# A transformer block with an expert gather: the V row of a step weighed before or after the dense work of that step

## The chip, the cores and the metric

The kernel runs on one core of one Trainium2 chip. The metric is the device time of one execution in microseconds. The kernel before took 2209.41 us, the median of three runs (2208.9 to 2215.3).

## The reference

The program is one residual block over 256 tokens of width 2048, all in float32: a token mixer (stick-breaking attention beside a gated linear recurrence), a layer norm, and then PEER, a channel mixer that picks experts by product keys. Only PEER matters here:

```python
q = (hf @ w_q).reshape(n_tok, PEER_HEADS, 2, PEER_HALF)
half_scores = jnp.einsum('thpd,hpnd->thpn', q, sub_keys)
s_top, i_top = lax.top_k(half_scores, PEER_TOPK)          # 16 of 128, twice
best, pos = lax.top_k(cand, PEER_TOPK)                    # 16 of 256 sums
gates = jax.nn.softmax(best, axis=-1)
act = jnp.einsum('td,thkd->thk', xb, u_tab[ib])           # gather of U rows
w = gb * jax.nn.gelu(act, approximate=False)
out = jnp.einsum('thk,thkd->td', w, v_tab[ib])            # gather of V rows
```

Each of 256 tokens picks 16 of 16384 experts in each of 8 heads. Its output is the sum of the V rows of these experts, weighed by gate times GELU of the product of its own row with the expert's U row. Scaled, the result is added to the residual and normed.

## The kernel before

The span has two parts. Up to about 1000 us come the modulation, the mixer and the query; they are not touched. Then comes the gather stage.

Tokens stand in two blocks of 128, one token to a partition. A *gathered row* is one choice of one head for one block: 128 experts, one per partition, 8 KB each. There are 2 x 8 x 16 = 256 such rows of U and as many of V. A step is named (n, e): n counts the 16 pairs of block and head, e the 16 choices. GpSimd issues the gathers as indirect DMAs (`gather_row`, L543): in step (n, e) the U row (n, e), then the V row (n-1, e). Each kind has a ring of five slots. A U row waits until VectorE has reduced the row that sits in its slot; a V row waits until TensorE has weighed the row in its slot. GpSimd's queue is in order, so a V row that waits holds back the U rows behind it.

VectorE reduces a U row to one number per token (`reduce_row`, L1568, 2.29 us). Once a head's 16 numbers are there, ScalarE takes their GELU (L724) and VectorE multiplies in the gates and spreads the weights over a matrix (`weigh`, L1579). TensorE weighs a V row with four narrow matmuls side by side in the array (`weigh_row`, L1128). At the start of each head it waits for the spread weights (`pe.wait_ge(s_wgt, n)`, L1224), ahead of all the work of that head's steps.

The gather serves only experts of the first 88 of 128 key rows; those of the last 40 key rows are out of the gather's bounds and are computed densely for all tokens. Three kinds of dense work are woven into the steps of TensorE's last loop by tables made from shares:

- `dense_u_piece` (L1150): one quarter of the product of a tile of 128 dense U rows with all tokens. There are 4 x 40 pieces, two in a step from (1,13) to (4,15), about one from (5,0) to (8,11). The tiles come on SP's queue (L491) into two slots. ScalarE takes their GELU (L763, L769).
- `spread_gates` (L1188): one matmul per token that puts its gates into a matrix of dense experts, from a column mask (made for even tokens by ScalarE, L787 and L788, for odd ones by VectorE, L1641) and a row mask (VectorE, L1633). Four tokens in each step from (5,0) to (8,15). Ahead of them stand two transpositions at the start of n = 5 (L1174, L1175), whose result ScalarE copies (L780).
- `dense_v_piece` (L1162): the weighed sum over the dense V rows, from step (9,4) on.

VectorE multiplies the dense activations with these gates (`weigh_dense`, `mix`).

The order of each engine's queue is that in which the code is written. The stretch of TensorE up to step (8,15) is called here the first stretch (n = 1 to 4, dense U pieces alone) and the masked stretch (n = 5 to 8, with gate matmuls).

Of the kernel before, what the change touches and what calls it, by code (L numbers as in the profile page):

```python
# [147 lines left out]
def block_kernel(nc, consts, x_rows, x_t, cond_cols, ada_early, ada_late, bias_cols, bias_late, w_early, weights, lb_logits, norm_gain,  # L148
                 ln_cols, ln_rows, subkeys_t, expert_u, expert_v, dense_u, x_mid, mod2, out):
    with ExitStack() as ctx:  # L150
# [217 lines left out]
        def v_expert(n, e):  # L368

            return (FIRST_OF_BANKS + [x for x in range(TOPK) if x % QUADS])[e] if n == HEADS else e  # L370

        def v_place(n, e):

            row = n * TOPK + e
            if n < BLOCKS * HEADS - 1:
                return v_slot[row % V_RING], v_used[row % V_RING], v_loaded[row % V_RING], row // V_RING
            if e % 2 == 0:
                row = n * TOPK + e // 2
                return v_slot[row % V_RING], v_used[row % V_RING], v_loaded[row % V_RING], row // V_RING
            row = (n + 1) * TOPK + e // 2  # L380
            return u_slot[row % U_RING], u_used[row % U_RING], u_loaded[row % U_RING], row // U_RING
# [200 lines left out]
        def _(act_e):  # L582
# [154 lines left out]
            def experts_to_quads(i):  # L737

                b, _, end = BATCHES_OF_HEADS[i]
                act_e.wait_ge(s_ex, b * HEADS + end)  # L740
                batch_to_quads(expert_q, expert, i).then_inc(s_exq, 1)

            def gates_to_quads(i):

                b, _, end = BATCHES_OF_HEADS[i]
                act_e.wait_ge(s_gl, b * HEADS + end)
                batch_to_quads(gates_q, gates_left, i).then_inc(s_gq, 1)
# [129 lines left out]
        def _(pe):  # L877
# [243 lines left out]
            def weigh_row(n, e):  # L1121

                slot, slot_used, slot_loaded, turn = v_place(n, e)
                e = v_expert(n, e)
                g = e // QUADS
                pe.wait_ge(slot_loaded, 16 * (turn + 1))
                for j in range(QUADS):
                    last = mm(ps[j * GROUP:(j + 1) * GROUP, n // HEADS * QUADS + g, :], spread_w[n % 2][:, e, :],  # L1128
                              slot[:, j * QCOLS:(j + 1) * QCOLS],
                              start=n % HEADS == 0 and e % QUADS == 0, stop=False, skip_group_check=True)  # L1130
                last.then_inc(slot_used, 1)

            def turn_stats(turn, groups):

                pe.wait_ge(s_stat, turn + 1)
                for a in groups:
                    last = mm(ps[:, a, 0:QUADS * 6], mean_quads, wide_rows[:, a % (QUADS + 1)], start=True, stop=True, skip_group_check=True)
                last.then_inc(s_turned, 1)


            def dense_u_piece(i):

                a, q = i // 4, i % 4
                if q == 0:
                    pe.wait_ge(dense_loaded[a % 2], 16 * (a // 2 + 1))
                    if a > 1:
                        pe.wait_ge(s_dact, a - 1)
                tile = dense_slot[a % 2].rearrange("p (k j) -> p k j", k=KT)
                for k in range(4 * q, 4 * q + 4):
                    last = mm(ps[:, 4 + a % 2, 0:TOKENS], tile[:, k, :], h2_t[:, k, :], start=k == 0, stop=k == KT - 1)  # L1150
                if q == 3:
                    last.then_inc(dense_used[a % 2], 1)

            def dense_v_piece(i):

                a, q = i // 4, i % 4
                t = DENSE + a
                if q == 0:
                    pe.wait_ge(dense_loaded[t % 2], 16 * (t // 2 + 1))
                for r in range(2 * q, 2 * q + 2):  # L1160
                    for j in range(QUADS):
                        last = mm(ps[j * GROUP:(j + 1) * GROUP, r, :], dense_act[a // 16][:, a % 16, r * GROUP:(r + 1) * GROUP],  # L1162
                                  dense_slot[t % 2][:, j * QCOLS:(j + 1) * QCOLS], start=False, stop=False, skip_group_check=True)
                if i == 4 * DENSE - 1:
                    last.then_inc(s_dv, 1)
                elif q == 3:
                    last.then_inc(dense_used[t % 2], 1)

            def transpose_choice(b):

                if b:
                    pe.wait_ge(s_slot, b)
                for c in range(2):
                    nc.tensor.transpose(ps[:, 6, c * P:(c + 1) * P], halves_of[:, c, b, :], ident)  # L1174
                nc.tensor.transpose(ps[:, 6, 2 * P:3 * P], gates[:, b, :], ident).then_inc(s_tok, 1)  # L1175

            def spread_gates(t):

                i = t // BATCH
                if t % BATCH == 0:  # L1180
                    pe.wait_ge(s_rowm, i + 1)
                    if i > 1:
                        pe.wait_ge(s_dw, i - 1)
                if t % 2 == 0:
                    pe.wait_ge(s_col, t // 2 + 1)
                else:
                    pe.wait_ge(s_colv, t // 2 + 1)
                mm(ps[:, 6 + i % 2, t % BATCH * DENSE:(t % BATCH + 1) * DENSE], col_mask[:, t % MASKS], row_mask[i % 2][:, t % BATCH, :],  # L1188
                   start=True, stop=True, skip_group_check=True).then_inc(s_gmm, 1)
# [33 lines left out]
            for n in range(1, BLOCKS * HEADS + 1):  # L1223
                pe.wait_ge(s_wgt, n)  # L1224
                if n == FIRST_MASKS:
                    pe.wait_ge(s_gt, BLOCKS * HEADS)
                    for b in range(BLOCKS):
                        transpose_choice(b)
                    pe.wait_ge(s_slot, BLOCKS)
                if n == HEADS + 1:  # L1230
                    pe.wait_ge(s_dw, BATCHES)
                for e in range(FIRST_BESIDE if n == 1 else 0, TOPK):
                    weigh_row(n - 1, e)
                    for i in DENSE_U_AT.get((n, e), ()):
                        dense_u_piece(i)
                    for t in TOKENS_AT.get((n, e), ()):
                        spread_gates(t)
                    for i in DENSE_V_AT.get((n, e), ()):
                        dense_v_piece(i)
                    if n == BLOCKS * HEADS and e == 5:  # L1240
                        turn_stats(0, range(QUADS))
                    if n == BLOCKS * HEADS and e in (6, 10, 14):
                        turn_stats(e // QUADS, [QUADS + e // QUADS - 1])
# [3 lines left out]
        def _(dve):  # L1247
# [335 lines left out]
            def add_to_rows(turn, groups):  # L1583

                dve.wait_ge(s_xq, 16)
                dve.wait_ge(s_dv, 1)
                for a in groups:
                    b, g = a // QUADS, a % QUADS
                    _, slot_used, _, turn_of_slot = v_place(b * HEADS + HEADS - 1, (g + 1) * QUADS - 1)
                    dve.wait_ge(slot_used, 2 + turn_of_slot)  # L1590
                    me.link(v.tensor_tensor(xo[:, b, g], ps[:, a, :], gate2q, ALU.mult))
                    me.link(v.scalar_tensor_tensor(out=xo[:, b, g], in0=xq[:, b, g], scalar=ALPHA, in1=xo[:, b, g], op0=ALU.mult, op1=ALU.add))
                    me.link(v.bn_stats(q_stats[:, a], xo[:, b, g]))
                    last = v.tensor_tensor(wide_rows[:, a % (QUADS + 1)].rearrange("p (j n) -> p j n", j=QUADS), q_stats[:, a].unsqueeze(1).to_broadcast([P, QUADS, 6]),
                                           own_quad.unsqueeze(2).to_broadcast([P, QUADS, 6]), ALU.mult)
                    if a < groups[-1]:
                        me.step(last)
                last.then_inc(s_stat, 1)
# [178 lines left out]
```

## Time and profile before

| | |
|---|---|
| median of three runs | 2209.41 us |
| profiled execution | 2206.26 us |
| its span | 2204.6 us |
| mean granted TensorE clock | 0.96 |
| TensorE busy | 1985.1 us (90%) |
| VectorE busy | 1364.3 us (62%) |
| GpSimd busy | 821.7 us (37%) |
| moved by DMA | 706.42 MB |

The profile is of one execution. Busy times are of the whole span; the stages of it have different limits, so most readings below are of a stretch. The DMA share is how busy the core's 16 DMA engines were in the mean; it can come out a little over 1. A time in brackets behind a row of the timeline is how long the engine sat idle before it, and the arrow names what ended the idle time.

### The profile page before, as it was taken

What the parts mean: (1) busy time and instruction counts of PE and PEld (TensorE: products, weight loads), DVE (VectorE), ACT (ScalarE), POOL (GpSimd) and SP (SyncE); (2) the same over time, 40 slices, a digit from 0 to 9 for tenths busy, and PEclk for the clock granted to TensorE, in tenths of its full rate; (3) what the DMA queues carried; (4) which work ended last, traced back from release to release, by engine and by line L of the source; (5) the groups of instructions that cost most, each with busy time, mean ns of one, the idle gap of its engine ahead of it and who ended that gap; (6) DMA issues with size and microseconds to landing.
All of it is one profiled execution on the core that took longest, in us unless ns stands there. A gap on an engine that the chain in (4) does not pass through costs nothing.

```text
span 2204.6 us, 29556 instructions
## 1 busy us (share of the span) xinstructions
PE 1985.1 (90%) x11435; PEld 1361.2 (62%) x11435; DVE 1364.3 (62%) x2099; ACT 388.2 (18%) x1020; POOL 821.7 (37%) x556
## 2 busy tenths in 40 slices
PE   4899999999999999989899999989887888888786
PEld 3788788888888888878656666666552222222221
DVE  7831377886544541148698879777885545555557
ACT  0122122221000001012132221644440000000001
POOL 1000000000000000005566455777787766667663
PEclk9999999999999999999999999999996999999997
DMA  9973356674765656319899999999999999999997
GB/s 384 428 314 115 153 220 271 271 302 196 286 282 228 247 210 252 150 58 342 332 362 414 404 410 409 350 406 379 393 378 369 405 403 407 373 412 412 405 406 281
DMA packets 106773, 706.42 MB, mean 320 GB/s; under 512 B 34227, under 2 KB 34259, under 8 KB 36323
## 3 DMA queue, kind: packets, MB, share of 16 engines
q0 software_dynamic: 78832, 432.67, 49.8%
q1 hardware_dynamic: 27826, 272.22, 30.8%
q8 instruction: 71, 1.16, 0.2%
q14 instruction: 44, 0.36, 0.0%
HBM read 875.16 MB, written 4.21 MB: 399 GB/s over the span
## 4 chain that ended last, share of the span: by engine, by line
PE 55%; DMA 28%; issue 6%; DVE 6%; POOL 3%; ACT 2%; SPq 0%; POOLq 0%; DVEq 0%
PE ps L884 24%; DMA arena<-expert_u,expert 18%; PE ps L892 10%; PE ps L1150 7%; DMA arena<-expert_v,expert_q 6%; PE ps L908 4%; PE ps L1128 3%; POOL arena L543 2%; DVE arena L1568 2%; PE ps L1204 2%; DMA arena<-dense_u 2%; PE ps L998 1%; DMA arena<-ada_early 1%; DMA mod_rows<-expert_v,expert_q 1%; DMA mod_rows<-expert_u,expert 1%
## 5 line engine op out<-in xcount | busy, mean ns | idle before, releaser
L1568 DVE CUSTOM_DVE_ANT_0 arena<-arena,buf_b 128x2048 f32<-128x2048 f32 x205 | 470.0, 2293 | 260.1 <-DMA arena<-expert_u,expert 258.7
L884 PE MATMUL ps<-buf_a,arena 128*128 128x256 f32 x1920 | 420.9, 381 | 0.9 <-ACT arena L626 0.9
L543 POOL DMA_INDIRECT arena<-expert_v,expert_q x206 | 342.0, 1660 | 162.5 <-PE ps L1128 76.4
L884 PEld LDWEIGHTS ps<-buf_a,arena 128*128 128x128 f32 x1920 | 365.3, 191 | 50.6 <-issue 1.2
L543 POOL DMA_INDIRECT arena<-expert_u,expert x205 | 307.0, 1498 | 156.3 <-DVE work L1568 56.8
L1128 PE MATMUL ps<-arena,mod_rows 128*32 128x512 f32 x1648 | 232.1, 640 | 114.0 <-DMA arena<-expert_v,expert_q 90.8
L1150 PEld LDWEIGHTS ps<-arena 128*128 128x128 f32 x1280 | 240.2, 195 | 132.9 <-issue 91.7
L1150 PE MATMUL ps<-arena 128*128 128x256 f32 x1280 | 315.8, 397 | 6.6 <-DMA arena<-dense_u 5.9
L531 POOL DMA_DIRECT2D arena<-ada_late x32 | 16.9, 529 | 744.3 <-DVE mod_rows L1322 615.8
L1128 PEld LDWEIGHTS ps<-arena,mod_rows 128*32 128x32 f32 x1648 | 36.9, 111 | 221.1 <-DMA arena<-expert_v,expert_q 154.0
L724 ACT ACTIVATE work<-work 32x4 f32<-32x4 f32 (+3 forms) x320 | 66.3, 207 | 538.3 <-DVE work L1568 530.9
L1568 DVE CUSTOM_DVE_ANT_0 mod_rows<-mod_rows,buf_b 128x2048 f32<-128x2048 f32 x51 | 116.9, 2292 | 67.8 <-DMA mod_rows<-expert_u,expert 67.6
L1322 DVE SCALAR_TENSOR_TENSOR mod_rows<-arena,cols,mod_rows 128x4096 f32<-128x4096 f32 x32 | 143.4, 4482 | 14.1 <-DMA arena<-ada_late 11.1
L1162 PE MATMUL ps<-arena 128*32 128x512 f32 x1024 | 125.1, 624 | 0.0
L1162 PE MATMUL ps<-arena,buf_a 128*32 128x512 f32 x1024 | 121.7, 610 | 0.0
L892 PE MATMUL ps<-arena,buf_a 128*128 128x256 f32 x512 | 112.3, 379 | 0.0
L884 PE MATMUL ps<-arena 128*128 128x256 f32 x512 | 111.8, 379 | 0.0
L892 PE MATMUL ps<-arena,buf_b 128*128 128x256 f32 x512 | 111.7, 379 | 0.0
L892 PEld LDWEIGHTS ps<-arena,buf_b 128*128 128x128 f32 x512 | 97.1, 190 | 15.7 <-issue 2.8
L884 PEld LDWEIGHTS ps<-arena 128*128 128x128 f32 x512 | 97.3, 190 | 13.2
L892 PEld LDWEIGHTS ps<-arena,buf_a 128*128 128x128 f32 x512 | 96.9, 190 | 13.0
L908 PE MATMUL ps<-buf_a,arena 128*128 128x256 f32 x384 | 91.9, 402 | 12.3 <-ACT buf_a L599 12.3
(258 smaller groups left out, 2060.6 us busy)
## 6 DMA issues: line engine op xcount, KB each, us to landing
arena<-weights SPq DMA_DIRECT2D x62, 2048.0 KB, 8.8
arena<-ada_late POOLq DMA_DIRECT2D x32, 2048.0 KB, 10.5
arena<-dense_u SPq DMA_DIRECT2D x40, 1024.0 KB, 9.1
arena<-expert_v SPq DMA_DIRECT2D x40, 1024.0 KB, 8.9
arena<-ada_early SPq DMA_DIRECT2D x16, 2048.0 KB, 17.4
arena<-w_early SPq DMA_DIRECT2D x8, 1536.0 KB, 9.3
arena<-expert_v,expert_q POOLq DMA_INDIRECT x206, 17.5
arena<-expert_u,expert POOLq DMA_INDIRECT x205, 17.6
```

What stands on the lines that cost most here:

```text
L543: pool.indirect_dma_start(slot, None, table, bass.IndirectOffsetOnAxis(ap=indices[:, n // HEADS, column:column + 1], axis=0), bounds_check ...
L724: last = run(target(k, g), source(k, g), function)
L884: last = mm(ps[:, bank, c * TOKENS:(c + 1) * TOKENS], ring[slot][:, first + k, c * P:(c + 1) * P], rhs[:, k, :], start=(k == 0), stop=(k = ...
L892: last = mm(ps[:, bank, b * COLS:(b + 1) * COLS], lhs[:, k, b * P:(b + 1) * P], ring[slot][:, k, :], start=(k == 0), stop=(k == KT - 1))
L908: last = mm(ps[:, c // 2, c % 2 * TOKENS:(c % 2 + 1) * TOKENS], early_slot[g % 2][:, k, c * P:(c + 1) * P], h_t[:, 2 * g + k, :], start=fi ...
L998: last = mm(ps[:, bank + n // 4, n % 4 * P:(n % 4 + 1) * P], decay[:, n, m], decay[:, n, m], start=True, stop=True)
L1128: last = mm(ps[j * GROUP:(j + 1) * GROUP, n // HEADS * QUADS + g, :], spread_w[n % 2][:, e, :], slot[:, j * QCOLS:(j + 1) * QCOLS], start= ...
L1150: last = mm(ps[:, 4 + a % 2, 0:TOKENS], tile[:, k, :], h2_t[:, k, :], start=k == 0, stop=k == KT - 1)
L1162: last = mm(ps[j * GROUP:(j + 1) * GROUP, r, :], dense_act[a // 16][:, a % 16, r * GROUP:(r + 1) * GROUP], dense_slot[t % 2][:, j * QCOLS: ...
L1204: last = mm(ps[:, 6 + s, i // 2 * TOKENS:(i // 2 + 1) * TOKENS], ring[s][:, k, i // 2 * P:(i // 2 + 1) * P], h2_t[:, k, :], start=k == 0, ...
L1322: v.scalar_tensor_tensor(out=sums, in0=ada_slot[s], scalar=cond[:, ds(k, 1)], in1=sums, op0=ALU.mult, op1=ALU.add).then_inc(ada_used[s], 1)
L1568: v.tensor_tensor_reduce(out=u_slot[s], in0=u_slot[s], in1=h2[:, n // HEADS], scale=1.0, scalar=0.0, op0=ALU.mult, op1=ALU.add, accum_out= ...
```

## The change

In each step of TensorE's last loop `weigh_row` moves behind the dense U pieces and the gate matmuls of the same step. The dense V pieces stay behind it. The wait for a head's spread weights stays ahead of all.

```diff
                 for e in range(FIRST_BESIDE if n == 1 else 0, TOPK):
-                    weigh_row(n - 1, e)
                     for i in DENSE_U_AT.get((n, e), ()):
                         dense_u_piece(i)
                     for t in TOKENS_AT.get((n, e), ()):
                         spread_gates(t)
+                    weigh_row(n - 1, e)
                     for i in DENSE_V_AT.get((n, e), ()):
                         dense_v_piece(i)
```

The first place is the start of the stretch on TensorE, steps (1,12) to (1,15). L1128 is a V row, L1150 are two dense U pieces (8 pairs of weight load and matmul in the program's count), L1195 the last transposition ahead of the loop.

```order
-L1128 MATMUL ps<-arena,mod_rows 32x512 x8
-L1150 MATMUL ps<-arena 128x256 x8
-L1128 MATMUL ps<-mod_rows 32x512 x4
-L1150 MATMUL ps<-arena 128x256 x8
-L1128 MATMUL ps<-arena,mod_rows 32x512 x4
-L1150 MATMUL ps<-arena 128x256 x8
+L1128 MATMUL ps<-arena,mod_rows 32x512 x4
+L1150 MATMUL ps<-arena 128x256 x8
+L1128 MATMUL ps<-arena,mod_rows 32x512 x4
+L1150 MATMUL ps<-arena 128x256 x8
+L1128 MATMUL ps<-mod_rows 32x512 x4
+L1150 MATMUL ps<-arena 128x256 x8
```

The V rows of steps (1,12) and (1,13) stood side by side (8 matmuls); now the pieces of (1,13) stand between them, and from there on each V row comes one set of pieces later.

The second place is the start of the masked stretch on TensorE, the last step of n = 4 and the first two of n = 5. L1174 and L1175 are the transpositions, L1188 the gate matmuls. This is the order before:

```order
274 L1128 MATMUL ps<-arena,mod_rows 32x512 x4
275 L1150 MATMUL ps<-arena 128x256 x12
276 L1174 MATMUL ps<-cst 128x128 x2
277 L1175 MATMUL ps<-cst,mod_rows 128x128
278 L1174 MATMUL ps<-cst 128x128 x2
279 L1175 MATMUL ps<-cst,mod_rows 128x128
280 L1128 MATMUL ps<-mod_rows 32x512 x4
281 L1188 MATMUL ps<-mod_rows 128x40 x4
282 L1128 MATMUL ps<-arena,mod_rows 32x512 x4
283 L1150 MATMUL ps<-arena 128x256 x4
284 L1188 MATMUL ps<-mod_rows 128x40 x4
```

And this is the order of the changed kernel there:

```order
275 L1150 MATMUL ps<-arena 128x256 x12
276 L1128 MATMUL ps<-arena,mod_rows 32x512 x4
277 L1174 MATMUL ps<-cst 128x128 x2
278 L1175 MATMUL ps<-cst,mod_rows 128x128
279 L1174 MATMUL ps<-cst 128x128 x2
280 L1175 MATMUL ps<-cst,mod_rows 128x128
281 L1188 MATMUL ps<-mod_rows 128x40 x4
282 L1128 MATMUL ps<-mod_rows 32x512 x4
283 L1150 MATMUL ps<-arena 128x256 x4
284 L1188 MATMUL ps<-mod_rows 128x40 x4
285 L1128 MATMUL ps<-arena,mod_rows 32x512 x4
```

The last V row of head n = 4 moved from before the three dense pieces to behind them, and the first of n = 5 from before the first four gate matmuls to behind them. TensorE's list has 690 such groups in both kernels. The lists of VectorE, ScalarE, GpSimd and SP are the same in both.

## Rows read from the trace of the kernel before

**Rows 1.** The page's section 4, the chain that ended last, by engine

```profile
PE 55%; DMA 28%; issue 6%; DVE 6%; POOL 3%; ACT 2%; SPq 0%; POOLq 0%; DVEq 0%
```

**Rows 2.** Windows: length, busy PE, PEld, DVE, ACT, POOL (instructions), granted clock, DMA share, GB/s

```profile
1130.00:1390.00 260.00, 248.31 (x1254) 164.72 (x1254) 222.40 (x559) 70.59 (x196) 142.99 (x106) 0.98 1.01 410
1395.00:1430.00 35.00, 33.50 (x206) 22.69 (x199) 31.15 (x60) 22.83 (x68) 30.53 (x15) 0.97 0.89 318
1430.00:1640.00 210.00, 192.67 (x1179) 132.76 (x1178) 167.69 (x336) 97.31 (x270) 162.87 (x100) 0.94 0.99 388
1640.00:1665.00 25.00, 12.93 (x74) 7.30 (x73) 14.36 (x30) 8.65 (x30) 18.94 (x13) 0.63 1.01 408
1720.00:2150.00 430.00, 352.25 (x3064) 93.93 (x3060) 223.11 (x203) 19.66 (x96) 295.10 (x190) 0.98 1.00 403
```

**Rows 3.** Timeline (start, length, engine, line), TensorE, first stretch: two steps, the last row

```profile
1147.23 1.06 PE L1128 MATMUL ps<-arena,mod_rows 128*32 128x512 f32 x8
1148.22 3.72 PE L1150 MATMUL ps<-arena 128*128 128x256 f32 x16
1151.88 1.06 PE L1128 MATMUL ps<-arena,mod_rows 128*32 128x512 f32 x8
...
1381.38 1.06 PE L1128 MATMUL ps<-arena,mod_rows 128*32 128x512 f32 x8
```

**Rows 4.** Timeline, TensorE, masked stretch: V rows of two steps in turn

```profile
1603.81 1.06 PE L1128 MATMUL ps<-mod_rows 128*32 128x512 f32 x8
...
1607.54 1.06 PE L1128 MATMUL ps<-arena,mod_rows 128*32 128x512 f32 x8
```

**Rows 5.** Timeline, several engines: from V row (1,10) to head 3

```profile
1198.34 1.07 PE L1128 MATMUL ps<-arena,mod_rows 128*32 128x512 f32 x8
...
1201.57 0.99 POOL L543 DMA_INDIRECT arena<-expert_u,expert  x1 [0.30 <-issue]
...
1223.51 2.30 DVE L1568 CUSTOM_DVE_ANT_0 arena<-arena,buf_b 128x2048 f32<-128x2048 f32 x1 [0.86 <-DMA arena<-expert_u,expert]
...
1229.02 0.69 DVE L1579 TENSOR_TENSOR mod_rows<-cst,work 128x512 f32<-128x512 f32 x1
...
1229.76 1.62 PE L1128 MATMUL ps<-arena,mod_rows 128*32 128x512 f32 x8 [2.92 <-DVE mod_rows L1579]
1231.31 4.81 PE L1150 MATMUL ps<-arena 128*128 128x256 f32 x16
```

**Rows 6.** Timeline, weight loads of the first V row of head 4

```profile
1309.01 0.16 PEld L1128 LDWEIGHTS ps<-arena,mod_rows 128*32 128x32 f32 x8 [0.33 <-DVE mod_rows L1579]
```

**Rows 7.** Line L543, gathers issued from 1400 to 1440 us, time to landing

```profile
DMA to landing us min/median/max: 8.2/10.1/12.8
```

**Rows 8.** Timeline, several engines: the start of the masked stretch

```profile
1390.78 1.94 PE L1128 MATMUL ps<-mod_rows 128*32 128x512 f32 x8 [1.04 <-ACT cst L780]
1390.83 0.49 DVE L1633 TENSOR_TENSOR mod_rows<-cst 128x320 f32<-128x320 f32 x1 [7.55 <-ACT cst L780]
...
1392.29 0.49 ACT L788 ACTIVATE mod_rows<-work,cst 128x128 f32<-128x128 f32 x1
...
1392.65 1.93 PE L1188 MATMUL ps<-mod_rows 128*128 128x40 f32 x8
...
1393.59 1.32 POOL L543 DMA_INDIRECT mod_rows<-expert_v,expert_q  x1 [7.99 <-PE ps L1128]
```

**Rows 9.** Waits from 1400 to 1640 us: total, times, longest

```profile
PE ps L1128 <- DMA arena<-expert_v,expert_q: 10.4, 6, 3.0
...
PE ps L1128 <- DVE mod_rows L1579: 4.1, 3, 2.0
```

**Rows 10.** Timeline, TensorE: V row (7,14) at the end of the masked stretch

```profile
1653.59 1.94 PE L1128 MATMUL ps<-arena,mod_rows 128*32 128x512 f32 x8 [6.91 <-DMA arena<-expert_v,expert_q]
```

**Rows 11.** Timeline, VectorE's dot product (7,3) and TensorE's V row of that step

```profile
1538.43 2.29 DVE L1568 CUSTOM_DVE_ANT_0 arena<-arena,buf_b 128x2048 f32<-128x2048 f32 x1 [2.33 <-DMA arena<-expert_u,expert]
...
1540.51 1.07 PE L1128 MATMUL ps<-mod_rows 128*32 128x512 f32 x8 [0.65 <-DMA mod_rows<-expert_v,expert_q]
```

## The prediction

> **What bounds the kernel now.** I read the page first, for what ended last over the whole span, then the windows of the gather stage, then the timeline of TensorE at three places, and last who waits for whom. On the page the chain that ended last belongs to TensorE for 55% and to DMA for 28% [rows 1]; that is a mean over stages. The edit acts only from step (1,12) of the last loop to step (8,15), about 1130 to 1660 us: from step (9,0) on, nothing stands between the V row and the dense V pieces and the order is as before.
>
> The windows split this stretch in three [rows 2]. From 1130 to 1390 TensorE is busy 248 of 260 us and DMA has share 1.01 at 410 GB/s: both are full. From 1395 to 1430 DMA falls to 0.89 and 318 GB/s: the one place where DMA has air. From 1430 to 1640 it is at 0.99 and 388 GB/s, slightly under the 410. Behind the edited part, 1720 to 2150, DMA runs at share 1.00 (403 GB/s) while TensorE has slack (352 of 430 us), so the end comes when DMA has moved a fixed number of bytes. What the edit is worth is therefore the DMA time that it wastes or saves before 1660 us, not what it does to TensorE.
>
> In the first stretch TensorE's own pace is 4.65 us a step: 1.07 for the V row, 3.72 for the two dense pieces, slightly overlapped [rows 3]. From row (1,0) at 1151.88 to row (3,15) at 1381.38, 47 steps, the mean is 229.5/47 = 4.88 us. So TensorE would ask 410 x 4.88/4.65 = 430 GB/s if nothing stopped it, and gets 410. In the masked stretch a step with one piece and four gate matmuls takes 1607.54 - 1603.81 = 3.73 us [rows 4].
>
> **The change, part by part.** Nothing is added or removed: 690 groups of matmuls stand on TensorE before and after, and the order of the other engines is the same word for word. The V row of a step moves behind the dense U pieces and the gate matmuls of its own step. Repeated, "V, U, gates" becomes "U, gates, V": the same cycle, so no matmul is dearer and the switches between narrow and full matmuls are as many. What changes is which V row stands beside which pieces, and so two loops:
>
> First, V row to gather. GpSimd issues V row r+5 when row r is weighed, and U rows stand behind it on its queue. The row now ends at the end of its step instead of 1.07 us into it, so relative to the dense pieces each gather is issued later by 4.65 - 1.06 = 3.6 us in the first stretch and 3.73 - 1.06 = 2.7 us in the masked one. From a V row to its own successor in the ring it is still five steps.
>
> Second, from a V row over the U gather, VectorE's dot product, GELU and the spread weights (L1579) to the wait at the next head. It has one part-step less of TensorE work to hide in.
>
> Term 1, first stretch. The second loop is tight already. At head 3 row (1,10) starts at 1198.34 and ends at 1199.4, the U row behind it is issued at 1201.57 and reduced at 1223.51, the spread weights come at 1229.02, and TensorE had waited 2.92 us for them [rows 5]. At head 4 the first weight load of the V row had 0.33 us of waiting for them and starts at 1309.01, just as TensorE is free: no slack [rows 6]. If all latencies stayed, the edit would add 3.6 us at each of these two heads. They don't stay: 22 us from issue to dot product is queueing in a full DMA (gathers issued from 1400 to 1440, with the queue short, land in 10.1 us at the median [rows 7]). A gather issued 3.6 us later into a queue that stays busy lands when it did before. So the landings, the spread weights and the wait keep their absolute times. I take 0. The bounds: -3, if the wait of 2.92 us goes because dense tiles and V rows wait less on one another; and +9, worked out in the first rival.
>
> Term 2, the start of the masks, 1382 to 1395. Here DMA runs dry, because GpSimd waits 7.99 us for V row (4,0), the first row of the new head [rows 8]. Before, that row runs from 1390.78 to 1392.72 while VectorE builds the row mask, and GpSimd issues at 1393.59. Now the gate matmuls of the step come first. They need the row mask (1390.83 + 0.49 = 1391.32), and the third token ScalarE's second column mask, 1392.29 + 0.49 = 1392.78. Two tokens can go from about 1392.0, the last two end near 1393.9 (the four took 1.93), and the row ends about 1393.9 + 1.94 = 1395.8: 3.1 us later than before. TensorE itself loses 1395.8 - 1394.6 = 1.2 us, GpSimd 3.1, and since DMA idles behind it this is lost for good. The dense pieces of step (4,15) also stand before row (3,15) now, but its gather is issued into a queue that is still full. I take +3; bounds 0 (GpSimd's own issues set the pace after it) and +5.8 (the 2.7 us of the later steps show here too).
>
> Term 3, the masked stretch, 1430 to 1640. Gathers are issued 2.7 us later relative to the pieces, out of some 22 us from issue to dot product [rows 5]: 12% less in the queue. DMA is (410 - 388)/410 = 5% under what it reaches when full, a sign that the queue is short at moments. If that shortfall grows in proportion, 5% x 12% x 210 us = 1.3 us; the gate matmuls' closer tie to VectorE can add to it, and I take +2. Bounds: -8 (second rival) and +8.1, three head waits grown by 2.7 each (before, the three are 4.1 us together [rows 9]).
>
> Term 4, the end of the masks. TensorE waits 6.91 us there for V row (7,14) with gate matmuls behind it [rows 10]; these now go first, and the last dense weights are ready earlier. But DMA is at share 1.01 from 1640 to 1665 [rows 2], so this frees engines that wait for DMA anyway: -1, bounds -3 and 0.
>
> Sum: 0 + 3 + 2 - 1 = +4 us. The profiled execution took 2206.3 us; it becomes 2210.3. The median of the runs shown is 3.15 us above it, so the forecast on that scale is 2209.4 + 4 = 2213 us.
>
> **A rule against this sum.** The rows show DMA at share 1.01 with 410 GB/s in the first stretch [rows 2]. The Trainium skill (DMA: Bandwidth & Descriptors, section "Where 436 GB/s comes from") puts the ceiling of the ports at 435 GB/s. By that ceiling the 430 GB/s asked for would fit, DMA would not be the bound, and the first rival would hold. The measured full rate speaks against it, so the ceiling moves a chance and not the sum.
>
> **The rivals.** (1) Head waits aren't absorbed: slower. If latencies stay as they are, the wait at the head grows by 3.6 at heads 3 and 4, and at heads 2 and 5 by between 0 and 3.6 (the traces show no wait there that I could add to; I take a third, 1.1 each), together 9.4; at heads 6 to 8 by 2.7 each, 8.1. With this TensorE stands still for over 6 us at head 3, and head 4 gets a wait like that of head 3 now, after which the row took 1.62 instead of 1.07 and the pieces 4.81 instead of 3.72 [rows 5], 1.6 us more. With terms 2 and 4 that is 9.4 + 8.1 + 1.6 + 2 = +21, less what any absorption gives: 2228. It decides once DMA's queue runs empty before the head's U row lands. For it: TensorE is the longest member of the chain; against it: share 1.01 in the same windows. The Trainium skill (TensorE: Matmul & The Clock Gate, "What's actually happening") says that an idle array falls to half clock; the slow row behind the 2.92 us wait agrees.
>
> (2) Faster. In the masked stretch TensorE waits 10.4 us for V rows in the arena slots with pieces and gate matmuls behind them [rows 9], and ScalarE and VectorE wait for gate matmuls. Now that work precedes the wait. If DMA's 5% shortfall there (about 11 us) comes from these stalls and two thirds go, -8 + 1 for the rest: 2202. Against it: each V wait still holds the next step's pieces, and its gather is issued later.
>
> (3) Masks come too late. VectorE's dot product of step (7,3) starts at 1538.43 and TensorE's V row of that step at 1540.5, a lead of 2.1 us [rows 11]; the column masks follow the dot product (2.29 us), and the gate matmuls now stand one row earlier. If a step grows from 3.73 to 3.9 us over 60 steps: +10 with the other terms +12, 2221.
>
> (4) Everything is hidden, 2209: counted with the forecast, for it lies within what can be told.
>
> **How the numbers follow.** Forecast with (4): 0.60, its own range 2206 to 2217. Rival 1: 0.20, rival 2: 0.11, rival 3: 0.09. A measurement of this kernel tells about 0.3% (6.6 us) from no change. Slower takes rivals 1 and 3 and a little of the forecast's upper edge, 0.31; faster most of rival 2, 0.09; same 0.60. The range from 2204 to 2226 leaves out the farther halves of rivals 1 and 2.
>
> **What would show it.** The wait before the first V row of heads 3 and 4 at about 3 and 0 us says that term 1 is absorbed; 6 and 3 say rival 1. GpSimd's gather behind V row (4,0) should start near 1396.7 instead of 1393.59, and DMA from 1395 to 1430 be below 318 GB/s. The share from 1430 to 1640 should be 0.98 to 0.99. A wait of L1188 on masks in most steps would show rival 3; V waits from 1400 to 1640 falling far under 10 us with a rise over 388 GB/s would show rival 2. I am wrong in the sum if the stage behind 1720 us doesn't simply shift.

## The result and the profile after

The changed kernel took 2216.34 us in the median (2209.31 to 2219.04, 20 runs), the kernel before 2208.85 us beside it (2204.11 to 2215.3, 20 runs). The ratio is 1.0030 with a 95% interval from 1.0021 to 1.0039: slower by 4.6 to 8.6 us (the two medians by themselves are 7.5 apart). The forecast was 2213 us and +4; the size lies at the upper edge of its own case, in the range, and just on the line that I had drawn between same and slower.

The profiled execution had a span of 2216.3 us, 11.7 more than before. Not all of that is the change. The first spread weights (VectorE, L1579) come ahead of the edited steps, and they are late already. These are the rows of heads 0, 1, 4 and 9 and of the last head in the kernel before (start, length, engine, line):

```profile
1072.12 0.69 DVE L1579 TENSOR_TENSOR mod_rows<-cst,work 128x512 f32<-128x512 f32 x1
...
1148.41 0.69 DVE L1579 TENSOR_TENSOR mod_rows<-cst,work 128x512 f32<-128x512 f32 x1
...
1382.59 0.69 DVE L1579 TENSOR_TENSOR mod_rows<-cst,work 128x512 f32<-128x512 f32 x1
...
1733.64 0.69 DVE L1579 TENSOR_TENSOR mod_rows<-cst,work 128x512 f32<-128x512 f32 x1
...
2166.70 0.75 DVE L1579 TENSOR_TENSOR mod_rows<-cst,work 128x512 f32<-128x512 f32 x1
```

And these in the changed kernel:

```profile
1078.17 0.69 DVE L1579 TENSOR_TENSOR mod_rows<-cst,work 128x512 f32<-128x512 f32 x1
...
1154.35 0.69 DVE L1579 TENSOR_TENSOR mod_rows<-cst,work 128x512 f32<-128x512 f32 x1
...
1390.71 0.69 DVE L1579 TENSOR_TENSOR mod_rows<-cst,work 128x512 f32<-128x512 f32 x1
...
1747.01 0.69 DVE L1579 TENSOR_TENSOR mod_rows<-cst,work 128x512 f32<-128x512 f32 x1
...
2178.66 0.69 DVE L1579 TENSOR_TENSOR mod_rows<-cst,work 128x512 f32<-128x512 f32 x1
```

The first is 6.05 us late, and it comes ahead of all that the diff touches. Each kernel has one profile: that of before is of an execution 2.6 us under its kernel's median, that of the changed kernel of one 1.6 us over. From head 0 to the last head it is 2178.66 - 1078.17 = 1100.5 against 1094.6, so +5.9 us, which agrees with the ratio; how much of the 6.6 us arises ahead of the first spread weights isn't shown by one profile of each. By stretches: heads 0 to 1 nothing (76.2 against 76.3), heads 1 to 4 +2.2 (236.4 against 234.2), heads 4 to 9 +5.3 (356.3 against 351.1), from head 9 on -1.4 (431.7 against 433.1). The windows that answer to [rows 2] are taken 6 us later, for the early lateness, and the last 12 us later (columns as there):

```profile
1136.00:1396.00 260.00, 248.02 (x1251) 165.06 (x1251) 222.12 (x559) 69.63 (x190) 151.37 (x104) 0.97 1.00 403
1401.00:1436.00 35.00, 33.99 (x201) 23.31 (x204) 28.75 (x57) 23.60 (x74) 23.85 (x16) 0.91 0.90 332
1436.00:1646.00 210.00, 195.83 (x1162) 133.30 (x1155) 165.42 (x329) 96.99 (x269) 160.41 (x97) 0.93 0.97 381
1646.00:1671.00 25.00, 14.10 (x91) 9.24 (x94) 16.96 (x33) 7.17 (x18) 20.92 (x13) 0.84 0.99 387
1732.00:2162.00 430.00, 352.40 (x3076) 95.01 (x3072) 224.98 (x203) 19.66 (x96) 295.38 (x190) 0.98 1.00 404
```

TensorE's busy time is the same within 1 us in the first window and the last; in the masked stretch it is 3.2 us longer. What fell is DMA: 403 for 410 GB/s in the first stretch, 381 for 388 in the masked one. The last stretch moves at the same rate as before. So the loss shows as bytes that DMA didn't move in time.

The first stretch shows where the queue went. These are rows on the gathers' line (L543) for 1230 to 1390 us, the idle time of GpSimd that a V row or a U row's reduction (L1568) ended (us, times) and the time from issue to landing, before:

```profile
  PE ps L1128: 33.8, 16
  DVE work L1568: 22.4, 8
...
DMA to landing us min/median/max: 12.2/16.7/23.0
```

And after:

```profile
  PE ps L1128: 49.3, 23
...
DMA to landing us min/median/max: 9.5/14.2/17.9
```

GpSimd waits 15.5 us longer for V rows, no longer waits for a U slot (22.4 us before), and what it issues lands 2.5 us sooner: the queue is shorter, as the prediction had it, and short enough to show. It shows at head 3. These are 20 us behind that point, at the same distance from the first spread weights, before:

```profile
1232.00:1252.00 20.00, 20.00 (x101) 13.55 (x100) 18.80 (x53) 3.55 (x5) 10.38 (x9) 0.96 0.99 390
```

And after:

```profile
1238.00:1258.00 20.00, 20.00 (x88) 14.11 (x88) 18.90 (x49) 3.55 (x5) 8.22 (x6) 0.87 0.93 356
```

Three places of the changed kernel answer to the prediction's. First, TensorE at the first dense tile, where V row (0,13) now stands behind the wait:

```profile
1143.51 5.74 PE L1150 MATMUL ps<-arena 128*128 128x256 f32 x16 [5.88 <-DMA arena<-dense_u]
1149.18 1.06 PE L1128 MATMUL ps<-arena,mod_rows 128*32 128x512 f32 x8
```

V row (0,13) ends at 1150.2. The prediction had not seen this: the row used to stand ahead of the wait for the tile. Behind it DMA runs at 370 GB/s, where it had 411 before (1140 to 1160 us):

```profile
1146.00:1166.00 20.00, 20.00 (x101) 13.54 (x100) 19.00 (x45) 8.75 (x26) 11.26 (x9) 0.96 0.96 370
```

Second, TensorE at head 3, which answers to [rows 5]:

```profile
1232.82 1.06 PE L1128 MATMUL ps<-arena,mod_rows 128*32 128x512 f32 x8
1237.99 6.29 PE L1150 MATMUL ps<-arena 128*128 128x256 f32 x16 [4.10 <-DVE mod_rows L1579]
1244.20 1.07 PE L1128 MATMUL ps<-arena,mod_rows 128*32 128x512 f32 x8
```

The wait grew from 2.92 to 4.10 us, not by 3.6, and now stands ahead of the dense pieces, which took 6.29 us instead of 4.81 behind it. At head 4 TensorE didn't wait for the spread weights. Third, the start of the masks, which answers to [rows 8]:

```profile
1398.83 0.49 DVE L1633 TENSOR_TENSOR mod_rows<-cst 128x320 f32<-128x320 f32 x1 [7.43 <-ACT cst L780]
...
1400.11 1.81 PE L1188 MATMUL ps<-mod_rows 128*128 128x40 f32 x8 [2.37 <-ACT mod_rows L788]
...
1401.84 1.94 PE L1128 MATMUL ps<-mod_rows 128*32 128x512 f32 x8
...
1404.65 0.99 POOL L543 DMA_INDIRECT mod_rows<-expert_v,expert_q  x1 [5.83 <-PE ps L1128]
```

From the row mask to the gather it is 1404.65 - 1398.83 = 5.82 us, before 1393.59 - 1390.83 = 2.76: 3.06 us later, where 3.1 had been worked out. But DMA's dip there is no deeper. The lowest of its stretches of 10 us before:

```profile
1400.00:1410.00 10.00, 8.50 (x56) 5.28 (x48) 7.77 (x20) 8.92 (x28) 8.78 (x5) 1.00 0.76 251
```

And in the changed kernel, 8 us later:

```profile
1408.00:1418.00 10.00, 8.99 (x59) 5.48 (x58) 8.29 (x19) 8.93 (x28) 6.77 (x5) 1.00 0.77 253
```

The waits of TensorE from 1400 to 1640 us before, beside those of [rows 9]:

```profile
PE ps L1128 <- DMA mod_rows<-expert_v,expert_q: 2.8, 3, 1.4
...
PE ps L1188 <- ACT mod_rows L788: 1.4, 1, 1.4
```

And its waits in the changed kernel from 1406 to 1646 us:

```profile
PE ps L1188 <- DVE mod_rows L1641: 7.6, 4, 2.8
...
PE ps L1188 <- DVE mod_rows L1633: 3.6, 5, 1.4
...
PE ps L1188 <- ACT mod_rows L788: 0.9, 1, 0.9
```

TensorE no longer waits for a V row there (10.4 + 2.8 = 13.2 us before), but 12.1 us for masks (1.4 before). One wait took the place of the other.

### The profile page after: what moved, and what is told of

Its sections match the earlier page's. It is cut to its first block, busy times and chain, and to the rows that moved or that the text cites. A ratio compares the mean times of both kernels' runs of the same rounds, so it can differ in the third digit from the quotient of the medians.

```text
span 2216.3 us, 29549 instructions
## 1 busy us (share of the span) xinstructions
PE 1992.9 (90%) x11435; PEld 1367.9 (62%) x11435; DVE 1364.6 (62%) x2099; ACT 388.5 (18%) x1020; POOL 821.3 (37%) x556
## 4 chain that ended last, share of the span: by engine, by line
PE 56%; DMA 27%; issue 6%; DVE 5%; POOL 4%; ACT 2%; SPq 0%; POOLq 0%; DVEq 0%
PE ps L884 24%; DMA arena<-expert_u,expert 12%; PE ps L892 10%; DMA arena<-expert_v,expert_q 8%; PE ps L1150 8%; PE ps L1128 4%; PE ps L908 4%; DMA mod_rows<-expert_u,expert 3%; POOL arena L543 3%; DMA arena<-dense_u 2%; PE ps L1204 2%; DVE arena L1568 1%; DMA arena<-ada_early 1%; PE ps L998 1%; DMA mod_rows<-expert_v,expert_q 1%
## 5 line engine op out<-in xcount | busy, mean ns | idle before, releaser
L1568 DVE CUSTOM_DVE_ANT_0 arena<-arena,buf_b 128x2048 f32<-128x2048 f32 x205 | 470.2, 2294 | 276.5 <-DMA arena<-expert_u,expert 273.2
L543 POOL DMA_INDIRECT arena<-expert_v,expert_q x206 | 346.0, 1680 | 192.8 <-PE ps L1128 130.2
L543 POOL DMA_INDIRECT arena<-expert_u,expert x205 | 300.8, 1467 | 148.6 <-issue 52.1
L1150 PE MATMUL ps<-arena 128*128 128x256 f32 x1280 | 320.2, 401 | 13.8 <-DMA arena<-dense_u 7.0
L1150 PEld LDWEIGHTS ps<-arena 128*128 128x128 f32 x1280 | 242.9, 197 | 140.2 <-issue 85.2
L1128 PE MATMUL ps<-arena,mod_rows 128*32 128x512 f32 x1648 | 231.3, 637 | 87.8 <-DMA arena<-expert_v,expert_q 71.4
L1128 PEld LDWEIGHTS ps<-arena,mod_rows 128*32 128x32 f32 x1648 | 37.2, 111 | 193.0 <-DMA arena<-expert_v,expert_q 129.8
L1568 DVE CUSTOM_DVE_ANT_0 mod_rows<-mod_rows,buf_b 128x2048 f32<-128x2048 f32 x51 | 117.0, 2294 | 61.5 <-DMA mod_rows<-expert_u,expert 61.3
L884 PEld LDWEIGHTS ps<-arena 128*128 128x128 f32 x512 | 97.3, 190 | 13.2
```

The lines of the kernel that those rows point to most:

```text
L543: pool.indirect_dma_start(slot, None, table, bass.IndirectOffsetOnAxis(ap=indices[:, n // HEADS, column:column + 1], axis=0), bounds_check ...
L884: last = mm(ps[:, bank, c * TOKENS:(c + 1) * TOKENS], ring[slot][:, first + k, c * P:(c + 1) * P], rhs[:, k, :], start=(k == 0), stop=(k = ...
L1568: v.tensor_tensor_reduce(out=u_slot[s], in0=u_slot[s], in1=h2[:, n // HEADS], scale=1.0, scalar=0.0, op0=ALU.mult, op1=ALU.add, accum_out= ...
```

## The experiments

All were timed in five rounds beside the kernel before; of ratios the 95% interval is given. Theory A at the start: the loss arises at two places, V row (0,13) behind the first tile (the expectations call it (1,13), by its step) and the start of the masks.

**The change in one stretch only.** `late` chooses where the V row goes in a step:

```diff
+                    late = n < FIRST_MASKS        # the other run: n >= FIRST_MASKS
+                    if not late:
+                        weigh_row(n - 1, e)
                     for i in DENSE_U_AT.get((n, e), ()):
...
-                    weigh_row(n - 1, e)
+                    if late:
+                        weigh_row(n - 1, e)
```

> The V row is weighed last only in the first stretch (steps (1,12) to (4,15), dense pieces alone); from (5,0) on the order is that of before. Theory A (the loss arises at two places: V row (1,13) now stands behind the wait for the first dense tile, and the start of the masks loses GpSimd's gather behind V row (4,0)): the first place alone remains, +2 to +3 us, ratio 1.0011, with DMA under 380 GB/s about 10 to 25 us behind row (1,13). Rival B (head waits that grow by a part-step each, nothing absorbed): +7 to +9 us, ratio 1.0035. Rival C (all of the loss is in the masked stretch): 0.

Measured: 1.0020 (1.0007 to 1.0034), median 2213.88 us.

> The V row is weighed last only from step (5,0) on; the first stretch is as before. Theory A: the loss at the start of the masks and a little in the masked stretch, +3.5 to +5 us, ratio 1.002. Rival B (head waits not absorbed): +8 us. Rival C (all of it here): +7, ratio 1.003. This run and the one with the first stretch alone should add up to the whole change (+6.6 us) if the places are independent.

Measured: 1.0011 (0.9997 to 1.0025), median 2211.56 us. The two add up to 1.0031, the whole change, as independent stretches would, though each interval is 3 us wide to either side. Theory C falls: the first stretch costs time, where I had forecast nothing. Which stretch costs more isn't shown. Rival B's 8 us for the masked stretch lies outside that run's interval (-0.7 to 5.5 us); its 7 to 9 us for the first stretch begin inside the other's (1.5 to 7.5 us).

**Undoing the two places.** `late` is `(n, e) > (1, TOPK - 3)` in the first run and `(n, e) != (FIRST_MASKS, 0)` in the second.

> The changed kernel, but steps (1,12) and (1,13) keep the order of before, so that V row (1,13) isn't behind the wait for the first dense tile. Theory A: 2 to 2.5 us of the loss come back, ratio to before 1.002. Rival B (the first stretch loses through the V rows' place in general, not through this one wait): no gain, 1.003.

Measured: 1.0036 (1.0020 to 1.0051). Nothing came back in the median (theory A's 1.002 is the very end of the interval), though the dip is gone. This is the same window of that run, with 416 GB/s for 370:

```profile
1146.00:1166.00 20.00, 20.00 (x105) 13.42 (x103) 18.82 (x50) 8.11 (x22) 10.98 (x10) 1.00 1.01 416
```

Nor does the dip belong to the order alone: the run with the first stretch changed has the same order here, and its profile shows 409 GB/s in this window.

> The changed kernel, but step (5,0), the first with gate matmuls, keeps the order of before, so that V row (4,0) doesn't wait for the masks. Theory A: 2 to 3 us come back, ratio to before 1.0018, and GpSimd's wait behind that row is shorter by some 2 us. Rival (GpSimd's own issues set the pace there): under 1 us comes back.

Measured: 1.0028 (1.0015 to 1.0042). At most a little came back; 2 to 3 us are near the interval's end (1.0015 for theory A's 1.0018). In both runs the rows behind the restored place are as late as in the changed kernel: where the order turns from early to late again, one V row stands behind two sets of dense work. The first run shows it, TensorE's timeline behind its two restored steps:

```profile
1138.68 8.80 PE L1150 MATMUL ps<-arena 128*128 128x256 f32 x32 [3.03 <-DMA arena<-dense_u]
1147.40 1.06 PE L1128 MATMUL ps<-mod_rows 128*32 128x512 f32 x8
```

Theory A found no support in either. Theory A2 took its place: what costs is that every V row ends later relative to the dense work; each gather is issued later, DMA's queue holds less, and DMA idles wherever it was short. The next three runs were to tell it from effects of place.

**The V row later still, and earlier.** The first puts each V row up to (8,15) off by one more whole step:

```diff
-                    weigh_row(n - 1, e)
+                    late_rows.append((n - 1, e))
+                    if n > HEADS or len(late_rows) > 1:
+                        weigh_row(*late_rows.pop(0))
+                    if (n, e) == (HEADS, TOPK - 1):
+                        weigh_row(*late_rows.pop(0))
```

> The changed kernel with each V row up to step (8,15) put off by one whole step more: it is weighed behind the dense work of the step after its own. Theory A2 (what costs is how late V rows end relative to the dense work: GpSimd's gathers are issued that much later, DMA's queue holds less, and DMA idles wherever the queue was short): the delay grows from 3.6 and 2.7 us to 8.3 and 6.4 us, so the loss is more than double that of the change, +15 to +25 us, with DMA clearly under full in the first stretch too (under 400 GB/s). Rival D (the loss comes from a few places where a V row newly stands behind a wait, the first dense tile and the first masks): +7 to +10 us.

Measured: 1.0127 (1.0103 to 1.0150), median 2235.58 us, +28 us by the ratio. The lateness is 2.3 times that of the change and the loss over four times: it grows faster than in proportion, which fits a queue that ran short now and then and now does so often. Its first stretch has 385 GB/s and DMA share 0.97, while its last runs at 402, close to all the others:

```profile
1130.00:1390.00 260.00, 240.70 (x1209) 160.79 (x1208) 216.12 (x549) 67.01 (x175) 145.31 (x101) 0.96 0.97 385
...
1720.00:2150.00 430.00, 358.55 (x3080) 95.30 (x3076) 223.66 (x202) 19.67 (x96) 296.84 (x192) 0.96 1.00 402
```

Rival D falls. The second keeps the V row first and puts the dense work of the step before behind it:

```diff
-                    for i in DENSE_U_AT.get((n, e), ()):
-                        dense_u_piece(i)
-                    for t in TOKENS_AT.get((n, e), ()):
-                        spread_gates(t)
                     weigh_row(n - 1, e)
+                    dense_of.append((n, e))
+                    while len(dense_of) > (0 if (n, e) == (HEADS, TOPK - 1) or n > HEADS else 1):
+                        at = dense_of.pop(0)
+                        for i in DENSE_U_AT.get(at, ()):
+                            dense_u_piece(i)
+                        for t in TOKENS_AT.get(at, ()):
+                            spread_gates(t)
```

> The opposite direction: the V row comes first in its step, and behind it the dense pieces and gate matmuls of the step before (in the kernel before it was those of the same step). Nothing is left out. Theory A2: gathers are issued 3.6 and 2.7 us earlier relative to the dense work, the queue is fuller, the dip at the start of the masks is smaller: -2 to -5 us against before, ratio 0.998 to 0.999. Rival D: 0 (only TensorE's order changes). Rival E (gate matmuls come too late for VectorE and ScalarE, which wait for them): +3 to +8 us.

Measured: 1.0020 (1.0008 to 1.0032), median 2212.24 us. The gain that A2 promised didn't come. Its one profiled execution is 0.6 us shorter than that of before from the first to the last spread weights (1094.0 against 1094.6), which doesn't explain a slower median. Its first spread weights come at 1076.19 us, 4.07 us later than before, ahead of all that was edited; whether that is this kernel or this execution isn't shown, and what costs here stays open. A gain does appear in the first stretch of the profile (232.4 us from head 1 to head 4, before 234.2) and is lost at the start of the masks (75.9 us from head 4 to head 5, before 73.7). So the sign of the rule holds on one side only: later is worse, earlier isn't better.

**The stretch around the masks.** `late` is `not ((FIRST_MASKS - 1, 10) <= (n, e) <= (FIRST_MASKS, 8))`.

> The changed kernel, but steps (4,10) to (5,8), around the start of the masks where DMA's queue runs short, keep the order of before. Theory A2: most of the loss that arises between the spread weights of heads 4 and 5 (3.1 us in the changed kernel's profile) comes back, ratio to before 1.0015 to 1.002. Rival F (the loss is spread evenly over the 116 steps): 26 of about 130 steps, 1.3 us come back, ratio 1.0027.

Measured: 1.0036 (1.0022 to 1.0049). Nothing came back, against A2 as it was put there and against rival F too. With the earlier two, three restored places gave nothing. That the double hold behind each restored place takes back what it gave is argued from the timeline above, and no run tests it.

**GpSimd's queue.** Here TensorE's order stays, in one run that of before and in one that of the changed kernel. Each U row is issued ahead of the V row that stood in front of it:

```diff
                     gather_u(n, e)
-                    if e == 0 and n in (2, 5, HEADS + 1):
-                        wait_alone(pool, s_exq, (2, 5, HEADS + 1).index(n) + 2)
-                    if n > 1:
-                        gather_v(n - 1, e)
-                    elif V_RING <= e + 1 < TOPK:
-                        gather_v(0, e + 1)
+                    if (n, e) != (1, 0):
+                        v_behind(*row_order[row_order.index((n, e)) - 1])
+            v_behind(BLOCKS * HEADS - 1, TOPK - 1)
```

`v_behind` holds the lines taken out.

> The kernel before with one edit on GpSimd's queue: each U row is issued ahead of the V row that stood in front of it (one place earlier), TensorE's order untouched. Theory A2 (a V row that isn't weighed yet holds back the U rows behind it): U rows are issued earlier, the queue is fuller in the dips, -2 to -4 us. Rival G (only the V rows' own gathers matter): 0 or a little slower, since V rows are issued behind one more U row.

Measured: 1.0012 (1.0002 to 1.0022), median 2210.69 us. By itself the edit is no gain, rather a small loss; A2 had that wrong.

> The changed kernel with the same edit on GpSimd's queue: each U row goes one place ahead of its V row. Theory A2: the loss of 6.6 us comes through the U rows held back, so at least half of it goes: ratio to before 1.000 to 1.0015. Rival G (it comes through the V rows' own later gathers): stays at 1.003 or more.

Measured: 1.0006 (0.9993 to 1.0019), median 2209.84 us. With the U rows out from behind the V rows, the two orders of TensorE are equal (2209.84 and 2210.69 us, 12 runs each; from their spread about 3 us either way, an estimate), where without it they are 6.6 us apart by the ratio. So the loss depends on what stands behind a V row in GpSimd's queue. The rows of L543 from 1230 to 1390 us in this run show what is different: GpSimd's wait for V rows is 25.3 us (49.3 in the changed kernel), it waits for U slots again, and the queue is long again.

```profile
  PE ps L1134: 25.3, 15
  DVE work L1574: 22.7, 9
...
DMA to landing us min/median/max: 13.0/18.7/26.0
```

Rival G falls: the V rows' own gathers are no earlier here, and its ratio of 1.003 or more is outside the interval. But the equality isn't that of every stretch. These are the spread weights of heads 1, 4 and 5 in the profile of before with the U rows ahead:

```profile
1152.27 0.69 DVE L1585 TENSOR_TENSOR mod_rows<-cst,work 128x512 f32<-128x512 f32 x1
...
1382.10 0.69 DVE L1585 TENSOR_TENSOR mod_rows<-cst,work 128x512 f32<-128x512 f32 x1
...
1461.64 0.69 DVE L1585 TENSOR_TENSOR mod_rows<-cst,work 128x512 f32<-128x512 f32 x1
```

The distances between spread weights, read in the same way from the one profile of each kernel, are these (us):

| kernel | heads 1 to 4 | heads 4 to 5 | heads 5 to 9 | first to last |
|---|---|---|---|---|
| before | 234.2 | 73.7 | 277.3 | 1094.6 |
| changed | 236.4 | 76.8 | 279.5 | 1100.5 |
| changed in the first stretch only | 236.1 | 75.5 | 278.0 | 1097.3 |
| changed in the masked stretch only | 233.9 | 75.5 | 277.9 | 1096.4 |
| V row a step later still | 247.9 | 76.4 | 288.1 | 1121.3 |
| before, U rows ahead | 229.8 | 79.5 | 276.6 | 1093.7 |
| changed, U rows ahead | 231.8 | 73.4 | 277.4 | 1091.6 |

In the first stretch the U rows' place is worth 4 to 5 us to either kernel, and the change still costs about 2 us there, as it does without it. The two orders come out equal because the kernel before loses its gain at the start of the masks, where the changed one doesn't. So the runs show that GpSimd's order decides whether the change costs time in the whole; that all of the loss goes through U rows held back isn't shown.

**The wait at the heads.** In the changed kernel the wait for the spread weights goes behind the first step's dense work for heads 2 to 4 and 6 to 8:

```diff
-                pe.wait_ge(s_wgt, n)
+                waits_behind = n in (2, 3, 4, 6, 7, 8)
+                if not waits_behind:
+                    pe.wait_ge(s_wgt, n)
...
+                    if waits_behind and e == 0:
+                        pe.wait_ge(s_wgt, n)
                     weigh_row(n - 1, e)
```

> The changed kernel with the wait for a head's spread weights put behind the first step's dense work, just ahead of its V row, for the six heads in which that is possible without touching the masks' start. Theory A2 (head waits are hidden anyway, since DMA is the bound): less than 1.5 us comes back. Rival B (head waits of TensorE cost end time; the profile has 4.10 us at head 3 and 2.6 us of pieces at half clock behind it): 5 us or more come back, ratio 1.001 or less.

Measured: 1.0049 (1.0031 to 1.0066), median 2217.79 us. No time came back, though at head 3 the wait of 4.10 us and the slow pieces are gone:

```profile
1233.43 3.72 PE L1150 MATMUL ps<-arena 128*128 128x256 f32 x16
1237.24 1.07 PE L1128 MATMUL ps<-arena,mod_rows 128*32 128x512 f32 x8
1238.24 3.72 PE L1150 MATMUL ps<-arena 128*128 128x256 f32 x16
```

DMA's dip at head 3 is gone with it (415 GB/s from 1237 to 1257 us, where the changed kernel has 356), but the gain didn't last: from head 1 to head 4 the profile takes 235.7 us for 236.4, from the first to the last spread weights 1100.3 for 1100.5. That is rival B's test, and it fails: taking these waits away brings nothing to the end.

> The kernel before with the first step of each of six heads in the other order: dense pieces, then the wait for the spread weights, then the V row, then the gate matmuls; all other steps as before. Theory A2: 0 to -1 us. Rival B (TensorE's waits at heads cost): -3 to -6 us.

Here the kernel before got the same wait, with pieces, wait, V row and gate matmuls in this order in the first step of the six heads. Measured: 1.0003 (0.9991 to 1.0014). No change, as A2 had it. No kernel tried here beats the one before.

## Why the prediction was right, and where not

**What bounds.** Right. The end follows DMA: over the last 430 us (1720 to 2150) all kernels run at 402 to 405 GB/s, TensorE's waits at the heads can be taken away and nothing comes of it, and what was lost ahead of that stays lost but for 1.4 us in the profile.

**Term 1, first stretch: 0, measured +2.2 in the profile and about 4.4 us (1.5 to 7.5) by the run with this stretch alone.** This is the step that was off. Its mechanism was half right: the wait at head 3 grew by 1.2 us and not by 3.6, head 4 had none, and the queue gave the rest (16.7 to 14.2 us from issue to landing). What failed is the sentence that the queue "stays busy". A share of 1.01 over 260 us is a mean; with the queue shorter by 2.5 us the mean fell to 1.00 and the rate from 410 to 403 GB/s, and in the 20 us at head 3 the share fell from 0.99 to 0.93. While TensorE waits there no V row is weighed, and GpSimd has 6 instructions in these 20 us for 9 before. That the queue runs short at a head was rival 1's condition, but of the 9.4 us that it put on heads 2 to 5 little came. I had also overlooked V row (0,13) behind the first tile, which the first rows of the order show at once; its dip stands in this profile, but the run without it gained nothing.

**Term 2, masks' start: +3.** The delay of 3.06 us for GpSimd behind V row (4,0) came as worked out from the rows. But that run's undoing gave back only 0.4 us by the ratios (with intervals of 3 us), so that the delay costs its full length at the end isn't shown. My reading of this window's rate as the sign was wrong: it rose from 318 to 332 GB/s, and the lowest 10 us of the dip are alike (251 and 253). From head 4 to head 5 the profile takes 3.1 us more, but the kernels with only one of the two stretches changed take 1.8 us more each, and with this step restored it takes 77.05 us; what makes up this part stays open.

**Terms 3 and 4, +2 and -1.** The masked stretch alone is +2.4 us (-0.7 to 5.5) against +4 for terms 2 to 4 together. The profile of the whole change has +5.3 us from head 4 to head 9. In it the V waits of rival 2 did vanish (13.2 to 0 us) and the mask waits of rival 3 did come (1.4 to 12.1 us); they nearly cancelled for TensorE, and DMA's rate went from 388 to 381 GB/s, its share from 0.99 to 0.97, under the 0.98 that was named as a sign. Term 4 has no run of its own.

**The sum: +4, measured +6.6 (4.6 to 8.6).** By the run with the first stretch alone, that stretch carries what was missing; by the profile, it is 2.2 us there and 1.3 us in the masked stretch less 1.4 us at the end. That the sum came as near as this is in part luck: term 1 was too low, and the time of term 2 came without the deeper dip that was to bring it. Rival 1 (+21) did not come, and with it fell the rule set against the sum: over 260 us of the first stretch no kernel moved more than 410 GB/s.

**What the prediction named and didn't use** is the second half of the first loop: "and U rows stand behind it on its queue". With that taken away the change costs nothing in the whole, though not in each stretch.

## What to carry to other kernels

An in-order queue that issues two kinds of transfer passes the lateness of one on to the other: before moving a consumer, look at what else stands behind its buffer's refill. A resource at share 1.00 absorbs a later issue only as long as its queue holds; price the shift against the queue's length at its shortest, and don't count on a cost in proportion (here 2.3 times the shift cost over four times as much). And undoing a shift at one place may tell little about that place, since the order must turn back somewhere and holds a row twice as long there.

## What the runs showed that I had not expected

Two profiles of code that is the same up to the edited steps differ by several microseconds ahead of them (6.05 us at the first spread weights; over all kernels tried these come between 1072.12 and 1078.17 us), so profiles are to be compared from an event ahead of the edited stage and not by their spans. And a stretch in which TensorE no longer waited for V rows was not faster: the wait for masks took its place almost whole (13.2 us of the one went, 10.7 us of the other came).
